# dt of a state-space layer: high and low weight parts side by side in one stationary tile, and the soft-plus on tokens

## The reference, cut to what matters

```
n = rms_norm(h, norm1_w[l])
proj = einsum('bld,de->ble', n, w_in[l])
z, xbc, dt_f, dt_b, sc_b, sc_c, sc_v = split(proj, SPLIT_POINTS)
...
dt = softplus(dt_raw + dt_bias)
a = -exp(a_log) * dt
xdt = xs * dt
a_cs = cumsum(a)        # within each chunk of 128 tokens
```

## Time and profile before

| what | value |
|---|---|
| time, median of 3 runs | 1676.11 us (1675.82 to 1676.83) |
| time of the profiled execution | 1675.97 us |
| its span, first to last instruction | 1674.1 us |
| TensorE matmul busy | 1656.4 us, 99% of the span |
| VectorE busy | 1325.9 us, 79% |
| ScalarE busy | 980.8 us, 59% |
| GpSimd busy | 71.6 us, 4% |
| mean granted TensorE clock | 0.998 |

### The profile page before, as it was taken

How to read it: one execution, slowest core, us unless ns; L and a number is a source line. 1 busy time by engine, 2 the same in 40 slices (tenths; PEclk the granted TensorE clock), 3 DMA queues, 4 the chain that set the end, 5 groups by cost and what they waited for, 6 DMA issues and landing times.

```text
span 1674.1 us, 26950 instructions
## 1 busy us (share of the span) xinstructions
PE 1656.4 (99%) x10635; PEld 1475.6 (88%) x10642; DVE 1325.9 (79%) x2061; ACT 980.8 (59%) x1631; POOL 71.6 (4%) x87
## 2 busy tenths in 40 slices
PE   9999999999999999999999999999999999999998
PEld 7999888888999978888899889888889988988886
DVE  6877678788877758878799988866679999786666
ACT  5576656666656846665644875544554487554444
POOL 2000000000200010000000011000000000100000
PEclk9999999999999999999999999999999999999999
DMA  7666546555566646555565554655647645466552
GB/s 239 184 197 191 184 155 201 191 187 164 178 179 205 193 164 197 194 192 186 165 213 177 171 178 160 208 190 188 194 139 220 210 143 177 164 201 201 190 189 100
DMA packets 237787, 308.09 MB, mean 184 GB/s; under 512 B 6531, under 2 KB 198749, under 8 KB 237661
## 3 DMA queue, kind: packets, MB, share of 16 engines
q1 hardware_dynamic: 237353, 306.26, 57.2%
q10 hardware_dynamic: 308, 0.12, 0.0%
HBM read 301.04 MB, written 1.11 MB: 180 GB/s over the span
## 4 chain that ended last, share of the span: by engine, by line
PE 91%; DVE 6%; issue 1%; ACT 1%; DMA 0%; POOL 0%; SPq 0%; POOLq 0%; DVEq 0%; ACTq 0%
PE ring_banks L544 68%; PE bank L544 17%; DVE weights_lo L1673 2%; PE bank L874 1%; DVE conv_sums L2098 1%; PE bank L981 1%; PE bank L992 1%; PE bank L834 0%; PE bank L1017 0%; DVE pair L2229 0%; PE bank L799 0%; DMA skips<-in_d_skip 0%; DVE queries_keys L2195 0%; DVE queries_keys L2232 0%; ACT weights_hi L1233 0%
## 5 line engine op out<-in xcount | busy, mean ns | idle before, releaser
L1673 DVE TENSOR_TENSOR weights_lo<-raw_weights,weights_hi 128x1024 fp32r<-128x1024 f32 (+1 forms) x550 | 643.3, 1210 | 105.4 <-ACT weights_hi L1233 104.4
L544 PE MATMUL ring_banks<-input_parts,weights_hi 128*128 128x256 f32 (+1 forms) x4000 | 691.2, 325 | 5.2 <-ACT input_parts L1282 1.9
L1233 ACT ACTIVATE weights_hi<-raw_weights 128x1024 fp32r<-128x1024 f32 (+1 forms) x552 | 544.3, 1036 | 185.1 <-PE bank L544 95.0
L544 PEld LDWEIGHTS ring_banks<-input_parts,weights_hi 128*128 128x128 f32 x4000 | 593.1, 190 | 66.9 <-issue 9.1
L544 PE MATMUL ring_banks<-input_parts,weights_lo 128*128 128x256 f32 x2752 | 373.8, 283 | 0.0
L544 PEld LDWEIGHTS ring_banks<-input_parts,weights_lo 128*128 128x128 f32 x2752 | 356.8, 192 | 7.3
L544 PE MATMUL bank<-weights_hi,hidden_hi 128*128 128x512 f32 x432 | 111.4, 392 | 0.0
L544 PE MATMUL bank<-weights_hi,hidden_lo 128*128 128x512 f32 x432 | 110.0, 389 | 0.0
L544 PE MATMUL bank<-weights_lo,hidden_hi 128*128 128x512 f32 x432 | 110.0, 389 | 0.0
L2098 DVE SCALAR_TENSOR_TENSOR conv_sums<-conv_padded,params_second_layer,conv_sums 128x256 f32<-128x256 f32 x240 | 99.2, 479 | 0.0
L544 PEld LDWEIGHTS bank<-weights_lo,hidden_hi 128*128 128x128 f32 x432 | 81.1, 188 | 16.8
(11 more groups left out here) (267 smaller groups left out, 1712.4 us busy)
## 6 DMA issues: line engine op xcount, KB each, us to landing
raw_weights<-in_w_in SPq DMA_DIRECT2D x103, 1024.0 KB, 5.4
raw_weights<-in_w_ff SPq DMA_DIRECT2D x64, 1024.0 KB, 5.3
raw_weights<-in_w_ffn_up SPq DMA_DIRECT2D x44, 1024.0 KB, 5.1
raw_weights<-in_w_ffn_down SPq DMA_DIRECT2D x22, 1024.0 KB, 4.9
raw_weights<-in_w_out SPq DMA_DIRECT2D x16, 1024.0 KB, 5.0
squares<-decay_rows SPq DMA_DIRECT2D x16, 512.0 KB, 4.9
raw_weights<-in_w_o SPq DMA_DIRECT2D x8, 1024.0 KB, 5.1
pair<-pair SPq DMA_DIRECT2D x64, 64.0 KB, 2.9
```

The source lines that it names most:

```text
L544: return mm(o, w, x, start=first, stop=last, skip_group_check=True)
L1233: A(whi[:, t, i * n:(i + 1) * n], raw[:, s, i * n:(i + 1) * n], ACT.Copy).then_inc(hi_done, 1)
L1673: tt(wlo[:, t, r], raw[:, s, r], whi[:, t, r].bitcast(f32), SUB).then_inc(w_ready, 1)
```

## The change

The dt chunk's 32 used columns are split into 32 high and 32 low ones that stand side by side in one stationary tile (`split_dt_hi`, `split_dt_lo`). One matmul of that tile with all 512 columns of `input_parts` gives the products with the high and the low input together, in 8 matmuls (`gemm_dt`). ScalarE copies the half for the low input out of PSUM (`dt_low`), VectorE adds the other half to it (`dt_sum`), TensorE turns the 64 rows to tokens in two transposes after chunk 2 (not 5), ScalarE copies the result (`dt_parts`), and VectorE adds its high and low columns. The soft-plus is then done on 128 partitions by 64 columns, two chunks later in the loops. Bias and a_log are no longer single rows that get transposed but are broadcast by four DMAs to all partitions (`dt_rows`). GpSimd writes dt and a straight to `dt_and_a_tokens`. The fourth product, low by low, is now part of the result.

More of the change, by code:

```diff
@@ L270, in build @@
         scale_rows = gates[:].rearrange("p a t -> p (a t)").rearrange("p (s d) -> p s d", d=D)
-        dts = sqb[0:32, 0:5, :]
-        dta = sqb[0:32, 5:7, :]
+        dt_sum, dt_low = sqb[0:64, 0, :], sqb[0:64, 1, :]
+        dt_parts = sqb[:, 2, 0:P].rearrange("p (t e) -> p t e", t=TOK)
+        dts = sqb[:, 2:4, :].rearrange("p a t -> p (a t)")[:, P:512].rearrange("p (i t e) -> p i t e", i=6, t=TOK)
+        dt_rows = diag[:, 0, :].rearrange("p (l i e) -> p l i e", l=DEPTH, i=2)
         sums = sqb[0:32, 2:4, :]
@@ L320, in build @@
         den_ready = sem("den_ready")
-        dt_dve, dt_act, dta_ready = sem("dt_dve"), sem("dt_act"), sem("dta_ready")
+        dt_dve, dt_act, dt_copied, dt_summed = sem("dt_dve"), sem("dt_act"), sem("dt_low_copied"), sem("dt_summed")
+        dt_rows_loaded, a_exp_ready, dt_turned = sem("dt_rows_loaded"), sem("a_exp_ready"), sem("dt_turned_copied")
         dtT, dtok_ready, cs_done, cs_ready = sem("dt_transposed"), sem("dtok_ready"), sem("cs_done"), sem("cs_ready")
@@ L905, in _ @@
                         u += 1
-                    if c == 5:
-                        pe.wait_ge(dta_ready, l + 1)
[L908 to L913, removed]
+                    if c == DT_CHUNK + 1:
[3 more added lines that the diff above has]
+                                                       kc[0:64, KC["ident"]:KC["ident"] + 64])
                         last.then_inc(dtT, 1)
@@ L1139, in soft_plus @@
             def soft_plus(l):
-                x, u, w, ln, one, den, a = [dts[:, i, :] for i in range(5)] + [dta[:, i, :] for i in range(2)]
+                x, u, w, ln, one, den = [dts[:, i] for i in range(6)]
+                dt, a = dtok[:, 0:2, :], dtok[:, 2:4, :]
                 pool.wait_ge(dt_dve, l * 2 + 2)
@@ L1156, in soft_plus @@
                 chain.sync()
-                chain(nc.gpsimd.tensor_tensor(den, den, x, ALU.add))
+                chain(nc.gpsimd.tensor_tensor(dt, den, x, ALU.add))
                 chain.sync()
-                nc.gpsimd.tensor_scalar(a, den, pc1[0:32, P1["a_exp"]:P1["a_exp"] + 1], -1.0, ALU.mult, ALU.mult).then_inc(dta_ready, 1)
+                chain(nc.gpsimd.tensor_scalar(one, dt, -1.0, None, ALU.mult))
+                chain.sync()
+                pool.wait_ge(a_exp_ready, 1)
+                nc.gpsimd.tensor_tensor(a, one, dt_rows[:, l:l + 1, 1, :].to_broadcast([P, TOK, 32]), ALU.mult).then_inc(dtok_ready, 1)
             chain = Chain(pool, pool_chain)
@@ L1233, in split_hi, with split_dt_hi @@
                     A(whi[:, t, i * n:(i + 1) * n], raw[:, s, i * n:(i + 1) * n], ACT.Copy).then_inc(hi_done, 1)
+            def split_dt_hi(cx, cr):
+                s, t = DT_CHUNK % RAW, DT_CHUNK % SPL
+                act.wait_ge(raw_loaded[s], cr * 16 + 16 * (DT_CHUNK // RAW + 1))
+                act.wait_ge(chunk_done, cx + (DT_CHUNK + 1))
+                for i in range(2):
+                    w, x = [b[:, j, 0:1024].rearrange("p (k n) -> p k n", k=8)[:, 4 * i:4 * i + 4, :] for b, j in ((whi, t), (raw, s))]
+                    A(w[:, :, 0:32], x[:, :, 0:32], ACT.Copy).then_inc(hi_done, 1)
             def multiplied(c, cx):
@@ L1289, in _ @@
                 input_hi(l * 2, "norm1")
-                split_hi(1, cx, cr, columns(list1, 1))
+                split_dt_hi(cx, cr)
                 if l == 0:
@@ L1673, in split_lo, with split_dt_lo @@
                     tt(wlo[:, t, r], raw[:, s, r], whi[:, t, r].bitcast(f32), SUB).then_inc(w_ready, 1)
+            def split_dt_lo(cx):
+                s, t = DT_CHUNK % RAW, DT_CHUNK % SPL
+                for i in range(2):
+                    dve.wait_ge(hi_done, cx * 2 + (2 * DT_CHUNK + i + 1))
+                    w, x = [b[:, j, 0:1024].rearrange("p (k n) -> p k n", k=8)[:, 4 * i:4 * i + 4, :] for b, j in ((whi, t), (raw, s))]
+                    tt(w[:, :, 32:64], x[:, :, 0:32], w[:, :, 0:32].bitcast(f32), SUB).then_inc(w_ready, 1)
             def split_quarter(c, cx, i):
@@ L1829, in _ @@
                 input_lo(l * 2, "norm1")
-                split_lo(1, cx, n=columns(list1, 1))
+                split_dt_lo(cx)
                 def outer_taps(dst, b, w, read):
@@ L1844, in outer_taps @@
                         last.then_inc(read, 1)
-                x, w, u_ = dts[:, 0, :], dts[:, 2, :], dts[:, 1, :]
+                x, w, u_ = dts[:, 0], dts[:, 2], dts[:, 1]
                 def heads_decayed(p, i):
@@ L1894, in extras @@
                 def extras(c):
+                    if c == DT_CHUNK + 1:
+                        dve.wait_ge(dt_turned, l + 1)
+                        chain(tt(x, dt_parts[:, :, 0:32], dt_parts[:, :, 32:64], ADD))
+                        chain.sync()
+                        dve.wait_ge(dt_rows_loaded, 16 * N_DT_ROW_DMAS)
+                        chain(tt(x, x, dt_rows[:, l:l + 1, 0, :].to_broadcast([P, TOK, 32]), ADD))
+                        chain.sync()
+                        stt(out=u_, in0=x, scalar=-1.0, in1=x, op0=MUL, op1=ALU.min).then_inc(dt_dve, 1)
                     if c in (7, 8):
```

8 lines of the change are left out of this document (2 added, 6 removed).

## The result

The changed kernel takes 1679.95 us (1678.46 to 1680.79), the kernel before on the same chip 1676.17 us: ratio 1.0022, 95% interval 1.0014 to 1.0029, or +3.78 us. The prediction had 1677.6 us, +1.5 us, in a range up to 1681.0; the interval, +2.3 to +4.9 us, leaves +1.5 out. The profiled execution took 1679.88 us with a span of 1678.1 us, 4.0 us longer than before.

What follows compares the result with a forecast made beforehand. TensorE, busy for 99% of the span, was taken to bound the kernel. Profiled 1675.97 us + 0.7 (waits, net of savings) + 0.8 (delayed input) = 1677.5, against the median 1677.6 us; range 1674.6 to 1681.0 us.

Steps and rivals of the forecast that it cites:

- The sum: Whole kernel: profiled execution 1675.97 us plus 0.7 and 0.8 us gives 1677.5; against the median 1677.6 us, +0.09%.
- likeliest case: Whole kernel: small losses from TensorE's new waits and the first microseconds, 1676.2 to 1678.9 us; chance 0.63.
- the start costs more: Rival, first microseconds: 64-byte runs at over twice 23 ns each, over +3 us, 1679 to 1681 us; chance 0.07.
- The shorter dt product: TensorE's dt chunk, each layer: 8 matmuls take 1.82 us instead of 2.88, 1.06 us less.
- The stall: TensorE behind chunk 2 waits for VectorE's sum, 1.7 us in layer 0, 1.25 in layer 1; net both layers +0.7.
- The transposes: TensorE, each layer: four after chunk 5, 0.44 and 0.45 us, go; two after chunk 2 cost 0.22 us.
- the ceiling: Most the change could gain if nobody waited: 1.28 us per layer, 2.6 us in all, 0.15%.
- The start: First 10 us: the four broadcasts' 1,024 runs share DMA engines with input x and delay it 0.8 us, between 0 and 1.5.
- The issue that blocks ScalarE: Rival, ScalarE's queue at the beginning: four slow broadcast issues delay the first weight split 7.8 us; 1684.6 us; chance 0.15.
- The clock: Rival: idle TensorE drops to 1.2 GHz for one chunk of one layer, 5.76 us more, 1683.4 us; chance 0.04.
- The soft-plus: Moved two chunks later on ScalarE, VectorE and GpSimd: ready by 52.4 us, TensorE asks at 52.8; costed at nothing.

Runs made afterwards that it cites:

- far addresses: Changed kernel with the four broadcasts replaced by 1,024 runs of 64 bytes read from far-apart places of w_in: 1676.68 us, ratio 1.0003.
- merged, late and early: Changed kernel with 512 runs of 128 bytes, broadcasts on SyncE's queue behind chunk 4's load, and VectorE's sum behind chunk 0's taps: 1674.31 us, ratio 0.9991.
- merged rows: Changed kernel with both layers' values of a tensor side by side, so 512 broadcast runs of 128 bytes instead of 1,024 of 64: 1676.81 us, ratio 1.0005.

## Why the prediction was right or wrong

The sum was 2.3 us short: +3.8 us measured, +1.5 forecast. The time lies above the likeliest case (1676.2 to 1678.9) and inside the range only because the range was drawn up to 1681 for the rival "the start costs more", which had a chance of 0.07. That rival's time came, but not its condition, packets at over twice 23 ns each: they took 8. So the hit on the range is in part luck. And +3.78 us is just over the 3.35 us below which the prediction saw the result with 0.77. Point by point:

- **The shorter dt product: right.** 1.83 us from dt to chunk 2 in layer 1, forecast 1.82.
- **The stall: right in mechanism, place and nearly in size.** Counted as the prediction counts, from 5.76 us behind the start of chunk 2, 1.50 and 1.16 us at the sum, forecast 1.7 and 1.25; 0.41 us for the sum itself, priced at 0.47. The late start has no part in it: with far addresses layer 0's is as long (1.27 us idle). From dt to chunk 6, layer 1 takes 451.27 - 424.89 = 26.38 us, before 447.44 - 421.07 = 26.37 (first line below): net 0.0, as forecast. With far addresses, where the start costs nothing, chunk 6 of layer 1 is 0.47 us late and the median 0.65 us up, against the forecast +0.7 for this term. Taking the stall away gave 2.7 us.
- **The transposes: a small miss inside it.** Two were put at 0.22 us, the four old ones at 0.45. First layer 1 of before, dt and the first product of the sums, which follows chunk 6; then chunks 2 to 4 and the same product in the merged, late and early kernel, where nobody waits:

```profile
421.07 2.08 PE L544 MATMUL bank<-input_parts,weights_hi 128*128 128x256 f32 x16
...
453.38 0.62 PE L842 MATMUL bank<-constants,dt_and_a_tokens 128*32 128x256 f32 x2
```

```profile
421.86 4.00 PE L552 MATMUL ring_banks<-input_parts,weights_hi 128*128 128x256 f32 x32
...
427.97 4.09 PE L552 MATMUL ring_banks<-input_parts,weights_hi 128*128 128x256 f32 x32
...
433.82 4.00 PE L552 MATMUL ring_banks<-input_parts,weights_hi 128*128 128x256 f32 x32
...
451.19 0.62 PE L860 MATMUL bank<-constants,dt_and_a_tokens 128*32 128x256 f32 x2
```

Chunk 3 begins 6.11 us after chunk 2 and chunk 4 5.85 us later: 0.35 us before the chunk behind the transposes and 0.09 us inside it, 0.44 in all. The old ones had 0.45 before chunk 6 and 0.09 us inside it as well (5.94 us up to the sums, 5.85 without transposes ahead), 0.54 in all. So two in the place of four save 0.10 us per layer, not 0.22, and the ceiling was 2 x (1.06 + 0.10) = 2.3 us, not 2.6. The first product of the sums comes 2.19 us early there.
- **The start: the step that failed, in price and in path.** "1,024 x 23 ns / 16 = 1.5 us on every engine" priced the runs by the time that packets keep an engine busy, and took 0.8 us of it for a delay of x. Measured, the start costs the difference between the whole and the far addresses, 3.78 - 0.65 = 3.1 us, twice the upper bound; the 11 times of the one lie wholly above those of the other. The runs were short in themselves (8 ns each); in the slow microseconds they came through at one per 9.3 ns for all engines together, and with other addresses at four times that rate. Nor did they act mainly where the prediction looked. VectorE took the last part of x at 7.92 us, 0.43 later than before. Over the profiled executions this time scatters: the four without broadcasts at the start have 7.01 to 7.49 us, 7.28 on average, the nine with them (shared bytes or not) 7.25 to 8.58, 7.84 on average. So half a microsecond may hang on x, of the 0.8 forecast. The rest went by what SyncE's queue issues and brings behind x, on which the prediction put nothing: it ended in the late parameter row and the late weights of chunk 2. By the rule of the Trainium skill that I cited (DMA: Bandwidth & Descriptors, Issuing engines are not separate DMA queues) transfers interleave, and the traces agree, 107 to 107 packets; that a queue that takes turns is slowed to the other's rate, I did not draw from it. The Trainium skill's 512 bytes (DMA: Bandwidth & Descriptors, Specifications), by which the prediction saw the start at the upper bound or over it, were not the cause: runs of 64 bytes went four times as fast from other addresses.
- **The issue that blocks ScalarE: did not come.** 0.49 to 0.72 us each. The 2.87 us of d_skip is not the price of the pattern: on the same queue, behind it, the four broadcasts took 0.60 to 0.79 us. That it stood for a full queue, as argued, fits this, but was not tested.
- **The clock: did not fall.** In the 2 us from 31 to 33, with TensorE busy for 0.71 us, the granted clock is 1.00, the 2.4 GHz level; the mean of the execution is 0.999.
- **The soft-plus: hidden, as costed.** GpSimd's last product, then what TensorE asks for:

```profile
53.13 0.33 POOL L1174 TENSOR_TENSOR dt_and_a_tokens<-squares,diagonals 128x64 f32<-128x64 f32 x1
```

```profile
56.13 0.62 PE L856 MATMUL bank<-constants,dt_and_a_tokens 128*32 128x256 f32 x2
```

2.7 us to spare, and its steps take 0.3 to 0.6 us instead of 2.38.

Not settled: whether it is the sharing or the place of these small tensors, and where in the path of a read the delay arises; why, with the broadcasts on SyncE's queue, the first some 700 small runs (d_skip's among them) passed at up to 358 per microsecond before the rate fell to 113; and why the queues do not always pass packets one for one (136 of SyncE's to 68 with merged rows from 11 to 12 us, 35 to 97 in the kernel before with the broadcasts from 14 to 15 us). The one broadcast of d_skip, 256 such runs, was in the kernel before and was not tried alone.

## What to carry to other kernels

A broadcast of a few bytes to 128 partitions is not priced by its bytes or by the engines' busy time: here 1,024 runs of 64 bytes, 256 on each of four pieces of 128 bytes, cost 3.1 us at a busy start and held up the queue beside them, while for 512 runs of 128 bytes the medians leave 0.1 us. So lay out its rows for one run per partition, or few. A low busy share of the DMA engines while a load is late is the sign to look for. And when a shortened step only brings TensorE sooner to a new wait, look where in its engine's order the awaited instruction stands: moving one sum of 0.41 us ahead of a weight split gave 2.7 us, more than the shortened matmuls themselves.

## What the runs showed of the hardware that was not expected

- The broadcasts' reads of 64 bytes came, once slow, at 70 to 120 per microsecond over all 16 DMA engines (107 in the view above), which they kept 3.5 to 6.5% busy; reads of the same size from different addresses, far or near, at up to 433 and 419 per microsecond beside as many packets of the other queue.
- Two queues of different engines passed packets nearly one for one in the changed kernel from 9 to 14 us (107 to 107) and with far addresses (433 to 436), and there the slower one set the rate of the faster: 61 GB/s instead of 278. In other kernels the counts differ, in both directions (Not settled, above).
- The pressure went back to the issuing engine: SyncE's issues of ordinary rows grew from 0.8 to 1.5 us each and from 0.36 to 1.91 us, while ScalarE's, which had caused it, stayed at 0.5 to 0.7 us.
